# Top-k masks moved behind the DeltaNet's preparation parts, two bisection steps per projection unit, and DeltaNet norms kept as columns

## The reference, cut to what matters

```
# gated DeltaNet, 4 heads of 128, 16 chunks of 64 tokens
q = l2norm(q) * 128**-0.5 ;  k = l2norm(k)         # l2norm: x * rsqrt(sum(x*x) + 1e-6)
kb = k * beta ; vb = v * beta
A  = strict_lower(kb k^T * gamma) ;  T = inverse(I + A)
u  = T vb ;  w = T (kb * exp(decay)) ;  qk = (q k^T) * gamma
scan over chunks: v_new = u - w S ; o = q_dec S + qk v_new ; S = S*last + k_dec^T v_new
o  = rms_norm(o, g_out) * silu(z)

# indexed sparse attention
score[t, s] = sum_h w[t,h] relu(q_idx[t,h] . k_idx[s])    over admissible s
keep the 256 highest s of each t (ties: the lower s first), softmax over these with an ALiBi bias
```

## Time and profile before

| | |
|---|---|
| median of 3 runs | 1887.45 us (1887.25 to 1892.19) |
| profiled execution, its own time | 1887.35 us |
| its span, first to last instruction | 1885.6 us |
| mean granted TensorE clock | 0.979 of full speed |
| busy: PE, DVE, ACT, POOL | 95%, 46%, 36%, 39% |

### The profile page before, as it was taken

How to read it: one execution, slowest core, us unless ns; L and a number is a source line. 1 busy time by engine, 2 the same in 40 slices (tenths; PEclk the granted TensorE clock), 3 DMA queues, 4 the chain that set the end, 5 groups by cost and what they waited for, 6 DMA issues and landing times.

```text
span 1885.6 us, 28354 instructions
## 1 busy us (share of the span) xinstructions
PE 1785.3 (95%) x11097; PEld 1432.0 (76%) x11097; DVE 863.9 (46%) x1426; ACT 677.9 (36%) x1418; POOL 726.1 (39%) x444
## 2 busy tenths in 40 slices
PE   6999989999988996899998998999999999999999
PEld 5888878777767883466786777888888888888887
DVE  4289868831383447566555356313221331222123
ACT  5366687797601323366215644100010001001000
POOL 4322135433334440256245126244334334333431
PEclk9999999999999998799998999999999999999999
DMA  7221111232230003000311001111111111111112
GB/s 231 63 72 27 31 34 45 53 104 90 90 112 2 3 3 134 12 1 2 135 45 45 23 12 45 45 56 45 46 54 44 55 34 56 52 48 44 55 34 89
DMA packets 112034, 102.44 MB, mean 54 GB/s; under 512 B 5131, under 2 KB 99390, under 8 KB 111678
## 3 DMA queue, kind: packets, MB, share of 16 engines
q1 hardware_dynamic: 109630, 92.67, 16.0%
q10 hardware_dynamic: 2304, 8.39, 1.1%
HBM read 87.42 MB, written 13.63 MB: 54 GB/s over the span
## 4 chain that ended last, share of the span: by engine, by line
PE 75%; DVE 15%; ACT 5%; issue 3%; SPq 1%; POOL 0%; DMA 0%; DVEq 0%; ACTq 0%; POOLq 0%
PE ps L1349 8%; PE ps L1351 8%; PE ps L1350 8%; PE ps L433 6%; PE ps L435 6%; PE ps L434 6%; PE ps L1058 3%; PE ps L405 3%; DVE cacc L1833 3%; PE ps L406 3%; PE ps L407 3%; PE ps L960 2%; PE ps L1180 2%; PE ps L1205 2%; PE ps L1191 2%
## 5 line engine op out<-in xcount | busy, mean ns | idle before, releaser
L737 POOL TENSOR_TENSOR WS<-WR,zero 128x1024 fp32r<-128x1024 f32 (+1 forms) x119 | 233.1, 1959 | 884.1 <-PE ps L407 304.9
L739 POOL TENSOR_TENSOR WS<-WR,WS 128x1024 fp32r<-128x1024 f32 (+1 forms) x119 | 307.5, 2584 | 9.3
L1349 PE MATMUL ps<-HS,WS 128*128 128x512 f32 x704 | 274.4, 390 | 3.2 <-DVE HS L341 3.2
L1351 PE MATMUL ps<-HS,WS 128*128 128x512 f32 x704 | 273.9, 389 | 0.0
L1350 PE MATMUL ps<-HS,WS 128*128 128x512 f32 x704 | 273.9, 389 | 0.0
L452 DVE TENSOR_TENSOR X<-X,ps 128x512 f32<-128x512 f32 x272 | 183.2, 686 | 155.7 <-PE ps L435 155.7
L405 PE MATMUL ps<-HS,WS 128*128 128x512 f32 (+2 forms) x592 | 228.0, 385 | 9.6 <-ACT raw L1473 7.6
L406 PE MATMUL ps<-HS,WS 128*128 128x512 f32 (+2 forms) x592 | 225.1, 380 | 0.0
L407 PE MATMUL ps<-HS,WS 128*128 128x512 f32 (+2 forms) x592 | 224.8, 380 | 0.0
L2102 DVE TENSOR_TENSOR prod<-sil,ps 128x512 f32<-128x512 f32 x44 | 30.2, 687 | 394.7 <-PE ps L1351 394.7
L1695 ACT ACTIVATE sil<-ps 128x512 f32<-128x512 f32 x44 | 26.3, 598 | 395.0 <-PE ps L1351 395.0
(11 more groups left out here) (313 smaller groups left out, 3032.0 us busy)
## 6 DMA issues: line engine op xcount, KB each, us to landing
WR<-in_w_gu SPq DMA_DIRECT2D x44, 512.0 KB, 3.8
WR<-in_w_in SPq DMA_DIRECT2D x36, 512.0 KB, 3.7
WR<-in_w_down SPq DMA_DIRECT2D x22, 512.0 KB, 3.5
X<-in_x SPq DMA_DIRECT2D x8, 1024.0 KB, 8.4
dsa_spill<-cacc ACTq DMA_DIRECT2D x12, 512.0 KB, 2.6
KW<-in_w_xkv SPq DMA_DIRECT2D x8, 512.0 KB, 4.9
WR<-in_w_out SPq DMA_DIRECT2D x8, 512.0 KB, 3.5
out<-X SPq DMA_DIRECT2D x8, 512.0 KB, 2.6
```

Of the source, the lines that this page charges most:

```text
L737: pool.tensor_tensor(hi, w, bc(zero1[:, 0:1], [P, cols]), ALU.add).then_inc(w_hi, 1)
L739: pool.tensor_tensor(lo, w, hi.bitcast(F32), ALU.subtract).then_inc(w_split, 1)
L1349: pe.matmul(ps[:, b0 + half, :], lo, HS[:, 0, k, c], start=(k == 0), stop=False)
L1351: mm = pe.matmul(ps[:, b0 + half, :], hi, HS[:, 0, k, c], start=False, stop=(k == KT - 1))
```

## The change

- `half_steps`: two half steps in each of the 12 units `u`, and the other 40 in 13 slots of `v` (three in each of the first twelve, four in the last).
- q and k stay unnormalised. The sums of squares are transposed once to columns (behind unit v = 11); DVE computes a few 128x32 tiles from them (`columns`): `bk2` = beta/|k|², `bk` = beta/|k|, used where beta was, and `eps_q`, which replaces the 1e-6 in the norm of o. The products of lines 999 and 1857 go, the root of line 1510 becomes a copy, and a root of 128x32 comes in unit v = 12.
- `kth_value` and `logit_bias` are cut into pieces and put behind the odd preparation parts (`threshold`, `MASKS`); three pieces of tile 7 and tiles 0 and 1 remain in chunks 12 and 13.
- Their scratch lies on ring slot 0 of `WS`; so the split of one w_out unit by POOL, and one later load by SP, come after the masks.
- The root for the norm of o waits for a small DVE product (`mean_o`), once before the meeting at the end of the scan.

```diff
         def half_steps(slot):
-            return range(2 * BITS * slot // SLOTS, 2 * BITS * (slot + 1) // SLOTS)
+            if slot < 12:
+                return range(2 * slot, 2 * slot + 2)
+            return range(24 + 40 * (slot - 12) // Z_SLOTS, 24 + 40 * (slot - 11) // Z_SLOTS)
@@ DSA_PARTS
-        {0: ("top", 0, 0), 1: ("top", 0, 0), 2: ("on", 0, 0), 3: ("sq", 0, 8), ...
+        {0: ("top", 0, 1), 1: ("top", 1, 2), 2: ("on", 0, 0), 3: ("sq", 0, 8), ...
@@ sync
-            for n in range(RING + 2, N_OUT + 2 * RING):
+            for n in range(RING + 2, N_OUT + 2 * RING - 1):
                 load(n)
...
             sp.dma_start(gB[:, :], g_xattn[0:1, :].to_broadcast([P, D])).then_inc(gB_in, 16)
+            load(N_OUT + 2 * RING - 1)
@@ gpsimd
-            for n in range(RING, N_OUT + RING):
+            for n in range(RING, N_OUT + RING - 1):
                 split_of(n)
...
             gdn_order(prep, lambda part, e0, e1: None, to_state=decayed)
+            pool.wait_ge(masks_made, 1)
+            split_of(N_OUT + RING - 1)
@@ tensor
-                if v >= 12:
-                    g0d.wait(pe, "rs")
...
-                        mm = pe.matmul(ps[:, 4 + e % 4, :], bc(pick(g, j), [32, P]), rsT[32 * g:32 * g + 32, :],
-                                       start=True, stop=True)
+                if v == 11:
+                    g0a.wait(pe, "rows")
+                    for k in range(4):
+                        mm = pe.transpose(ps[:, 6, k * P:(k + 1) * P], sqg[:, k * P:(k + 1) * P], ident[:, :])
@@ scalar
                 if v == 10:
                     g0p.wait(act, "st7")
-                    g0a.mark(act.activation(sdT[:, :], ps[:, 4, :], ACT.Sqrt, bias=eps_t[:, 0:1]), "sd")
+                    g0a.mark(act.activation(sqg[:, 0:BANK], ps[:, 4, :], ACT.Copy), "rows")
...
+                if v == 12:
+                    g0d.wait(act, "rk2")
+                    g0a.mark(act.activation(gtmp[:, 0:32], rk2[:, :], ACT.Sqrt), "rk")
...
             def o_rms(i, t0, t1):
-                ta.wait(act, f"q{t1 - 1}")
+                td.wait(act, f"e{i}")
@@ vector
+            def mask(t, stage):
+                n, q = (t + 1) * P, RANKED.index(t)
...
+                if stage == "count":
+                    above(t)
+                    rlink(dve.tensor_scalar(room, room, -1.0, float(TOPK), ALU.mult, ALU.add))
+                elif stage == "tie":
+                    rlink(dve.tensor_scalar(tie, s, V, None, ALU.is_equal))
+                elif stage in range(4):
+                    c0, c1 = 2 * P * stage, min(2 * P * (stage + 1), n)
+                    rlink(dve.tensor_tensor_scan(order[:, c0:c1], bc(ones1[:, 0:1], [P, c1 - c0]), tie[:, c0:c1],
+                                                 order[:, c0 - 1:c0] if stage else 0.0, ALU.mult, ALU.add))
+                elif stage == "kept":
+                    rlink(dve.scalar_tensor_tensor(tie, order, room, tie, ALU.is_le, ALU.mult))
+                elif stage == "out":
+                    rlink(dve.scalar_tensor_tensor(tie, s, V, tie, ALU.is_le, ALU.subtract))
+                else:
+                    rlink(dve.scalar_tensor_tensor(s, tie, -BIG, negdist[:, (TT - 1 - t) * P:SEQ], ALU.mult, ALU.add))
+            MASKS = {7: [(2, "count"), (2, "tie")], 9: [(2, 0), (2, 1)], 11: [(2, "kept"), (2, "out"), (2, "bias")],
+                     13: [(3, "count"), (3, "tie")], 15: [(3, 0), (3, 1)],
+                     17: [(3, "kept"), (3, "out")], 19: [(3, "bias"), (4, "count")], 21: [(4, "tie"), (4, 0)],
+                     23: [(4, 1)], 25: [(4, 2), (4, "kept")], 27: [(4, "out"), (4, "bias")],
+                     29: [(5, "count"), (5, "tie")], 31: [(5, 0), (5, 1)],
+                     33: [(5, 2)], 35: [(5, "kept")], 37: [(5, "out"), (5, "bias")], 39: [(6, "count")],
+                     41: [(6, "tie")], 43: [(6, 0)], 45: [(6, 1)], 47: [(6, 2), (6, 3)],
+                     49: [(6, "kept")], 51: [(6, "out")], 53: [(6, "bias")], 55: [(7, "count")], 57: [(7, "tie")],
+                     59: [(7, 0)], 61: [(7, 1)], 63: [(7, 2), (7, 3)]}
+            def threshold(p):
+                if p == 1:
+                    kth_flushed()
+                    above(7)
+                elif p == 3:
+                    for t in (2, 3, 6):
+                        above(t)
+                elif p == 5:
+                    above(5)
+                    above(4)
+                elif p == 7:
+                    kth_settled()
-            for v in range(SLOTS - 12):
-                if v == 10:
...
+            for v in range(Z_SLOTS):
+                if v == 12:
+                    columns()
                 for h in half_steps(12 + v):
                     rank(h)
-            kth_value()
-            for e0, t in ((0, 4), (4, 3), (8, 2)):
-                unit_norms(e0)
-                logit_bias(t, gB, rankA)
-            unit_norms(12)
             meet(2, dve)
...
+            def mean_o(i, t0, t1):
+                ta.wait(dve, f"q{t1 - 1}")
+                td.mark(dve.scalar_tensor_tensor(gtmp[:, 4 * t0:4 * t1], ss[:, 4 * t0:4 * t1], 1.0 / GD,
+                                                 eps_q[:, 4 * t0:4 * t1], ALU.mult, ALU.add), f"e{i}")
...
             def dsa(part, e0, e1):
                 if part == "on":
+                    mean_o(0, 0, T_ON)
                     scale_o(0, 0, T_ON)
-                elif part == "sq":
-                    for t in ((5, 0, 1, 6) if e0 == 0 else (7,)):
-                        logit_bias(t, vb[:, 0, :], wTt[:, 0, :])
+                elif part == "top":
+                    mask(7, "kept" if e0 == 0 else "out")
+                elif part == "sq" and e0 == 0:
+                    mask(7, "bias")
+                    for t in range(2):
+                        bias_only(t)
+                    dve.sem_inc(masks_made, 1)
...
+            def prep_and_masks(b, part):
+                p = len(PREP) * b + PREP.index(part)
+                prep(b, part)
+                threshold(p)
+                for t, stage in MASKS.get(p, ()):
+                    mask(t, stage)
-            gdn_order(prep, dsa, to_state=to_state)
+            gdn_order(prep_and_masks, dsa, to_state=to_state)
+            mean_o(1, T_ON, TT)
             meet(2, dve)
             scale_o(1, T_ON, TT)
```

More of the change, by code:

```diff
@@ L138, in build_layer @@
         erem = small("erem", 32)
+        bk = small("bk", 32)
+        bk2 = small("bk2", 32)
+        rk2 = small("rk2", 32)
+        eps_q = small("eps_q", 32)
         lastb = small("lastb", 64)
@@ L489, in build_layer @@
         LV = range(1, 6)
-        g0p = steps("g0_pe", ["sums"] + [f"st{u}" for u in range(8)] + [f"bc{e}" for e in range(16)])
+        g0p = steps("g0_pe", ["sums"] + [f"st{u}" for u in range(8)] + ["cols"])
         g0a = steps("g0_act", ["beta", "abs", "exp", "ln", "ea"] + [f"sq{u}" for u in range(8)]
-                    + ["sd", "ed", "erem", "last"])
-        g0d = steps("g0_dve", ["z", "max", "sp", "g", "rs", "nbed"] + [f"n{e}" for e in range(16)])
+                    + ["rows", "ed", "erem", "last", "rk"])
+        g0d = steps("g0_dve", ["z", "max", "sp", "g", "ek", "rk2", "eq", "bk2", "nbed", "bk"])
         gp = steps("gdn_pe", ["k0", "k1", "v0", "v1", "GQ", "diff", "db0", "db1", "x0"]
@@ L503, in build_layer @@
         T_ON = 6
-        td = steps("gpost_dve", ["r0"] + [f"on0{h}" for h in range(2)] + ["r1"] + [f"on1{h}" for h in range(2)]
+        td = steps("gpost_dve", ["e0", "r0"] + [f"on0{h}" for h in range(2)] + ["e1", "r1"] + [f"on1{h}" for h in range(2)]
                    + [f"y{i}" for i in range(TT)])
@@ L990, in _ @@
                     g0p.mark(mm, f"st{u}")
-                if v >= 12:
-                    g0d.wait(pe, "rs")
[L993 to L998, removed]
-                        mm = pe.matmul(ps[:, 4 + e % 4, :], bc(pick(g, j), [32, P]), rsT[32 * g:32 * g + 32, :],
-                                       start=True, stop=True)
-                        g0p.mark(mm, f"bc{e}")
+                if v == 11:
+                    g0a.wait(pe, "rows")
+                    for k in range(4):
+                        mm = pe.transpose(ps[:, 6, k * P:(k + 1) * P], sqg[:, k * P:(k + 1) * P], ident[:, :])
+                    g0p.mark(mm, "cols")
             meet(0, pe)
@@ L1556, in o_rms @@
             def o_rms(i, t0, t1):
-                ta.wait(act, f"q{t1 - 1}")
-                ta.mark(act.activation(gtmp[:, 4 * t0:4 * t1], ss[:, 4 * t0:4 * t1], ACT.Sqrt, bias=eps_t[:, 0:1],
-                                       scale=1.0 / GD), f"sd{i}")
+                td.wait(act, f"e{i}")
+                ta.mark(act.activation(gtmp[:, 4 * t0:4 * t1], gtmp[:, 4 * t0:4 * t1], ACT.Sqrt), f"sd{i}")
             def dsa(part, e0, e1):
@@ L1788, in rank @@
                     dve.tensor_scalar(cand[:, c], thr[:, c], 1 << (BITS - 2 - k), None, ALU.bitwise_xor).then_inc(rank_cand, 1)
[L1790 to L1805, removed]
@@ L1807, in logit_bias @@
```

(1 more changed line is left out.)

68 lines of the change are left out of this document (40 added, 28 removed).

## The result

The kernel before took 1888.01 us (median of 4 runs, 1887.25 to 1892.19), the changed one 1875.12 us (median of 4, 1872.48 to 1876.69). The ratio is 0.9926, 95% interval 0.9907 to 0.9944. The forecast was 1879.0 us, range 1870 to 1888.

The account below looks back on a forecast made before the run. PE was taken as the bound, busy 167.2 of 167.2 us in the projections' second half. From 1887.35 us, -7.3 - 3.05 + 1.3 - 4.15 + 5.6 + 2.3 - 3.3 = -8.6 gave 1878.75, forecast 1879 us, range 1870 to 1888.

Parts of the forecast that it names:

- Two half steps per unit u: Projections: PE's three stalls for ACT's copies go (5.7 us), with the half clock after the first (1.6): gain 7.3.
- Three half steps per unit v: Projections: ACT's 10.2 us of work fits in PE's 10.9 us unit, 0.7 to spare: no cost.
- Rival B: Projections: ACT becomes late in unit v, half a microsecond in each of 13 units eats the 7.3: 1886; chance 0.07.
- Columns: Projections: three groups of spreading products go (3.8 us), four transposes come (0.5 plus 0.25): gain 3.05.
- Table load: Block 0: the first Exp needs a load of ACT's table, on the chain from exponent to mask: cost 1.3.
- Meeting: Before the blocks: PE waits for the landing of ACT's last DMA instead of DVE: gain 4.15, bounds 2 and 4.2.
- Pieces behind decay: DeltaNet blocks: mask pieces run ahead of TT0, which y1 needs; 2.0, 1.5, 1.0 and 1.1: cost 5.6.
- POOL and DVE shutting each other out: DeltaNet blocks: pieces meeting POOL instructions exceed their windows, 0.5 to 0.6 us a block: cost 2.3, bounds 0 and 25.
- Rival A: Blocks: one POOL instruction's wait in each of 20 y windows, 25.4 in place of 2.3: 1902; above 1890, chance 0.10.
- Tail: Chunk 14 onward: the inverse and all behind come 3.9 earlier, `mean_o` costs 0.6: gain 3.3, bounds 0 and 3.9.
- C: Meeting bound by a landing of 5 us instead of 2.6: 1881.3; with the tail's gain lost 1884, in a 0.18 case.
- D: Blocks: pieces free but for decay and the load: 1876.5; with half of the decay pieces hidden 1873; chance 0.15.

Follow-up runs that it names:

- the kernel with the light tail: The kernel before, with the five top-k masks in chunks 12 to 15 replaced by plain copies of the distance bias: 1880.60 us, ratio 0.9965.
- the kernel with the three edits: The changed kernel with no mask pieces behind decay, the table loaded early and ACT's wait moved to POOL: 1866.35 us, ratio 0.9886 to before.

## Why the prediction was right, step by step

- **Two half steps per unit u, -7.3.** Right in mechanism, a little small: from the product behind the first stall to the start of unit v = 11 before takes 222.19 us (266.60 to 488.79), after 216.41 (261.53 to 477.94), and with the 2.30 of that stall it is 8.1. Of this 0.9 is hidden in the ledger, because the changed kernel's execution had half clock that much longer right behind the product where the stretch begins (25.06 against 24.19 without the stall). Undoing it costs 8.5, since the old spread in the new kernel stalls four times.
- **Three half steps per unit v, 0.** Right: PE is busy 156.10 of 156.10 us with them. Rival B is out.
- **Columns, -3.05.** Right in mechanism, -3.4 in size: three groups at 1.26 as said, but the transposes cost 0.46 and not 0.75. That the projections as a whole came out at -10.6 for -10.35 is in part luck: -8.1 - 3.4 + 0.9.
- **Table load, +1.3.** Right in mechanism and size: its row is 1.28 us (below) and its removal takes 1.27 off PE's wait. By the Trainium skill, "ScalarE: Activation LUTs", section "What ACT_TABLE_LOAD costs", it would have been about 2.7; no run here shows the drain in it.
- **Meeting, -4.15.** Right to the hundredth, bound by the landing as said: PE starts 2.75 us behind the issue of the last DMA, and with ACT's wait for it elsewhere PE's wait is 1.72. The DMA and the load in ACT's timeline:

```profile
534.28 0.33 ACTq L1505 DMA_DIRECT2D dsa_spill<-cacc  x1
545.39 1.28 ACT L1534 ACT_TABLE_LOAD   x1 [11.14 <-PE ps L1044]
```

- **Pieces behind decay, +5.6.** The mechanism is right, the size 4.7: 2.0, 1.2, 0.7 and 0.8. In blocks 2 and 3 the step was drawn wrongly: it is not TT0 that comes late but POOL's `gam`, held by the piece that started first:

```profile
635.95 1.01 DVE L1829 SCALAR_TENSOR_TENSOR tieW<-orderW,count,tieW 128x768 f32<-128x768 f32 x1
...
636.11 1.98 POOL L820 TENSOR_TENSOR gam<-Am,Lev 128x512 f32<-128x512 f32 x1 [1.23 <-DVE qdec L1956]
...
638.14 1.15 PE L1062 MATMUL ps<-TTm,gam 64*64 64x64 f32 x32 [1.36 <-POOL gam L820]
```

- **POOL and DVE shutting each other out, +2.3.** Right in kind, too large: about 1.4 in blocks 1 to 3 for the pieces in windows; in block 0 the clock covers it. Rival A (0.55 us a window and more) is out. The exclusion itself is plain: a running sum of 128 columns lasted 1.41 us and ended 0.3 behind POOL's instruction, where another of that size took 0.48; two counts of one size differ by 0.01 at most anywhere in the blocks. The Trainium skill has both, the exclusion and the exempt counting form, in "SBUF — State Buffer", section "Who interferes with whom". The trace agrees, with the numbers above.

```profile
567.06 1.26 POOL L820 TENSOR_TENSOR gam<-Am,Lev 128x512 f32<-128x512 f32 x1 [2.66 <-PE ps L1062]
567.20 1.41 DVE L1826 TENSOR_TENSOR_SCAN orderW<-ones,orderW,tieW 128x128 f32<-128x128 f32 x1
```

- **The moved split and its load, 0.** Right: nothing from the attention on is longer in the ledger.
- **What was missing: PE's clock in the blocks.** Block 1 took 3.15 more and not 2; 1.8 of it is half clock (42.01 against 40.22 in the same code). That the blocks sum to the forecast (+9.3 for 9.2) is two errors cancelling: about 1.8 too much for pieces and exclusion, 1.8 of clock left out. And block 0 of the kernel before takes 36.80 in one execution and 34.67 in another, so the sum itself stands to about 2 us. The prediction had priced half clock in the projections and never asked for it here, though the wait at y1 of block 0 (2.84) is longer than the 2.30 that stands ahead of half clock in the earlier trace rows.
- **Tail, -3.3.** It was -5.0. The inverse's part was -3.9 as said. `mean_o` cost 0.2 by the executions of before and after (spreading to the transposes of v 16.63 instead of 16.46), not 0.6; but that length is 15.93 in the kernel with the light tail, which has no `mean_o` either, so anything up to 0.7 is open. Its root took 0.21 us and not 0.30. And the second group of sums took 1.57 instead of 2.44: full clock came back earlier, which brought the third 0.64 forward. The wait ahead of the first was 3.27 and not 3.75. The changed rows, to set against the earlier trace rows:

```profile
732.64 0.68 ACT L1581 ACTIVATE sdH<-ps,eps_t 128x512 f32<-128x512 f32 x1
...
733.36 3.35 DVE L2014 RECIPROCAL rsH<-sdH 128x512 f32<-128x512 f32 x1 [0.89 <-ACT sdH L1581]
...
736.76 2.02 PE L1151 MATMUL ps<-rsH,ident 32*64 32x512 f32 x16 [2.99 <-DVE rsH L2014]
...
753.09 0.21 ACT L1566 ACTIVATE gtmp<-gtmp 128x8 f32<-128x8 f32 x1 [5.53 <-DVE gtmp L1988]
```

The terms give 1878.75, the profiled execution took 1872.48. Of the 6.3 between them 3.6 is the stretch ahead of the change, 1.7 the tail, 0.6 the attention, and the rest mostly the projections. So more than half of the miss is code that the change doesn't touch. Two sums among the rivals are slightly off: C is 1881.2 and not 1881.3, and D with half of the decay pieces hidden 1873.7 and not 1873.

## What to carry to other kernels

Work that fits into another engine's idle time costs little where it stands behind a wait that is long enough (here about 1.4 us in three blocks), and costs about its full length where it stands ahead of an instruction on the chain: place pieces by what follows them in program order, not by the engine's busy share (the same DVE work cost 9 us less two parts away, about half of it by the place itself and half by PE's clock). Compare two executions by lengths between marks behind the last shared stretch: the start of this comparison alone moved by up to 5.6 us. And where PE waits again and again for two or three microseconds, price the half clock behind the waits too, or give PE something to do in them. Gains that contain clock don't add.

## What the runs showed of the hardware

- PE's granted clock in a block can differ where the block's code does not: block 1 took 42.00 and 42.01 us in two executions of one kernel, 42.02 with three more groups in the projections, and 40.22 with the stalls there; block 0 of the kernel before took 36.80 and 34.67. What decides it is open. A wait of 1.72 us at the meeting left the next transposes at full clock (1.97 us); a wait of 3.90 was followed by 3.67 or 3.68 in four executions, by 3.18 and 3.38 in two, and by 1.97 in one.
- Six unused products of 128x256 in block 0's waits and three ahead of the meeting, put into the kernel with the three edits, held the clock at 1.00 through all blocks and took 2.5 us off block 0.
- Four products on four different groups of 32 rows and four banks took 1.07 us together, four on three groups and three banks 1.9.
- What excluded DVE and POOL was not tied to size: a POOL instruction of 1.26 us held a DVE one of 128 columns, to 1.41, and DVE's of 1.01 held a POOL one of 1.27, to 1.98.
